# Joining two attention passes into one software pipeline, with the rank projections moved ahead under the convolutions

## The reference

```
# first block; x is normalised, then projected once (weights in_proj)
cq, ckv, kpe, mq, mk, mv, mo, i_pre, f_pre = split(x_normed @ w_in)   # widths 256,128,64,512,512,512,512,4,4
# MLA: 4 heads, causal softmax
q = rms_norm(cq) @ w_uq          # per head 128 "nope" + 64 rotary columns
k, v = rms_norm(ckv) @ w_ukv     # 128 + 128 per head
q_pe, k_pe = apply_rope(q[..., 128:]), apply_rope(kpe)
ctx_mla = causal_mla(q, k, v)
# mLSTM: 4 heads of 128
mq, mk = silu(causal_dwconv(mq)), silu(causal_dwconv(mk))             # 4 taps
h = mlstm_chunkwise(mq, mk, mv, i_pre, f_pre)
h = rms_norm(h per head) * sigmoid(mo)
x = x + post_norm(concat(ctx_mla, h) @ w_out)
```

## Time and profile before

| | |
|---|---|
| Device time, 3 runs | 1392.2 us median (1389.93 to 1393.25) |
| The profiled execution's own time | 1387.27 us |
| Its span, first to last instruction | 1385.3 us |
| Mean granted TensorE clock | 0.983 of full speed |
| PE busy | 95% of the span |
| DVE busy | 57% |
| ACT busy | 40% |
| POOL busy | 3% |

### The profile page before, as it was taken

One profiled execution on the slowest core, in us unless ns is written; L12 is line 12 of the kernel. 1 busy time (PEld: TensorE's weight loads), 2 busy tenths in 40 slices (PEclk: granted clock), 3 DMA queues, 4 the chain that ended last, 5 costly groups with the idle time before them and its releaser, 6 DMA issues.

```text
span 1385.3 us, 17842 instructions
## 1 busy us (share of the span) xinstructions
PE 1316.9 (95%) x6548; PEld 1109.3 (80%) x6548; DVE 784.4 (57%) x1298; ACT 555.7 (40%) x914; POOL 44.9 (3%) x47
## 2 busy tenths in 40 slices
PE   7998879999999999999999999999899999999996
PEld 6877767789888888888777887878798788888886
DVE  5776767556644544222675797586685632355434
ACT  5645545534323223322454654555552322223221
POOL 3000000000000000000021000010000000000002
PEclk9999989999999999999999999999999999999999
DMA  5220110321232233333223232330211232222322
GB/s 177 92 92 16 54 46 16 99 69 61 92 100 97 91 97 113 109 106 106 91 91 107 91 99 84 92 92 31 92 62 61 92 107 91 91 97 100 106 92 76
DMA packets 37101, 120.46 MB, mean 87 GB/s; under 512 B 4508, under 2 KB 6556, under 8 KB 37040
## 3 DMA queue, kind: packets, MB, share of 16 engines
q1 hardware_dynamic: 36464, 117.98, 26.2%
q0 software_dynamic: 576, 1.65, 0.4%
HBM read 112.27 MB, written 2.11 MB: 83 GB/s over the span
## 4 chain that ended last, share of the span: by engine, by line
PE 77%; DVE 14%; ACT 4%; issue 3%; DMA 1%; POOL 0%; POOLq 0%; ACTq 0%; DVEq 0%; SPq 0%
PE bank L779 24%; PE bank L781 24%; PE bank L780 24%; DVE w_lo L1863 3%; DVE tiles L1863 2%; DVE tiles L1866 2%; DVE arena L1863 2%; DVE probsT L1863 1%; PE bank L923 1%; ACT w_hi L1327 1%; PE bank L885 1%; PE bank L876 1%; DVE arena L1866 1%; DVE negmax L2071 1%; ACT arena L1348 1%
## 5 line engine op out<-in xcount | busy, mean ns | idle before, releaser
L1863 DVE TENSOR_TENSOR w_lo<-raw_slab,w_hi 128x1024 fp32r<-128x1024 f32 x199 | 244.3, 1227 | 295.1 <-ACT w_hi L1327 279.7
L779 PE MATMUL bank<-u_hi,w_hi 128*128 128x512 f32 x852 | 337.8, 396 | 14.8 <-DVE tiles L1863 3.8
L781 PE MATMUL bank<-u_hi,w_lo 128*128 128x512 f32 x852 | 334.3, 392 | 0.0
L780 PE MATMUL bank<-u_lo,w_hi 128*128 128x512 f32 x852 | 334.2, 392 | 0.0
L1327 ACT ACTIVATE w_hi<-raw_slab 128x1024 fp32r<-128x1024 f32 x189 | 199.2, 1054 | 183.7 <-PE bank L781 179.9
L779 PE MATMUL bank<-arena,w_hi 128*128 128x512 f32 (+1 forms) x672 | 253.8, 378 | 9.7 <-DVE w_lo L1863 4.9
L780 PE MATMUL bank<-arena,w_hi 128*128 128x512 f32 (+1 forms) x672 | 251.8, 375 | 0.0
L781 PE MATMUL bank<-arena,w_lo 128*128 128x512 f32 (+1 forms) x672 | 251.8, 375 | 0.0
L779 PEld LDWEIGHTS bank<-u_hi,w_hi 128*128 128x128 f32 x852 | 161.2, 189 | 51.7 <-DVE tiles L1863 5.1
L781 PEld LDWEIGHTS bank<-u_hi,w_lo 128*128 128x128 f32 x852 | 161.3, 189 | 34.3
L780 PEld LDWEIGHTS bank<-u_lo,w_hi 128*128 128x128 f32 x852 | 161.4, 189 | 31.8
(11 more groups left out here) (221 smaller groups left out, 1564.7 us busy)
## 6 DMA issues: line engine op xcount, KB each, us to landing
raw_slab<-in_stream SPq DMA_DIRECT2D x207, 512.0 KB, 3.4
arena<-arena SPq DMA_DIRECT2D x32, 128.0 KB, 2.3
residual<-in_xT SPq DMA_DIRECT2D x8, 256.0 KB, 7.8
out_hT<-residual SPq DMA_DIRECT2D x16, 128.0 KB, 1.7
arena<-forget_rows SPq DMA_DIRECT2D x8, 128.0 KB, 2.3
tiles<-in_pT POOLq DMA_DIRECT2D x2, 256.0 KB, 3.0
tiles<-bias_rows POOLq DMA_DIRECT2D x1, 512.0 KB, 3.9
tiles<-in_positions POOLq DMA_DIRECT2D x1, 256.0 KB, 3.5
```

The lines of the kernel that those rows point to most:

```text
L779: pe.matmul(o, ws[0], xs[0], start=first, stop=False)
L780: pe.matmul(o, ws[0], xs[1], start=False, stop=False)
L781: return pe.matmul(o, ws[1], xs[0], start=False, stop=last)
L1863: return nc.vector.tensor_tensor(o, a, b, op)
```

## The change

1. The slabs `kpe` and `gates1` become one, `rg` (gate rows beside the rotary rows). The rotary half-swap, which before was a second set of weight columns, is done by DVE operations that read the other half of the partitions. One slab (24 matmuls) fewer.
2. The stream is now `mv`, `rg`, `cq0`, `cq1`, `ckv`, the eight convolution products in the order of heads (`CONV` = mq0, mk0, mq1, ...), `mo0`: 13 slabs after `mv`. Rank squares, stats and spreads, the rotary tables (`rotary_angles`, ten DVE operations, now before the first norm's `inverse_root`) and the rotary key lie on ACT, DVE and PE among them.
3. The two attentions are one `attention("first")` of 32 units in 38 steps. Fills: halves of `mo1..3` at steps 0 to 5, sixteen expansion products at steps 6 to 13 and 16 to 23, all in PSUM bank 7, one stat of all four mLSTM heads at step 24, four spreads at steps 26 to 29, and 24 matmuls of `out1` at steps 32 to 35. The interlude is gone. MLA's keys and values go to the place of the first block's input (`u_hi`, `u_lo`).
4. Slab conversions in the pipeline follow a table, `FIRST_CONVERT`: at a step it names the slab in use, and the one behind it is converted.

The core of the diff:

```diff
-PHASES = [("mv", 4), ("gates1", 1), ("mq", 4), ("mk", 4), ("mo0", 1), ("mo1", 1), ("mo2", 1), ("mo3", 1),
-          ("cq0", 1), ("cq1", 1), ("ckv", 1), ("kpe", 1), ("uqpe", 1), ("ukv", 1),
-          ("uq", 1), ("out1", KD + 4), ("glu_rest", 2 * KF1 - 4), ("down1", 3 * KD), ("proj", 2), ("ple", KD),
+CONV = [f"m{c}{h}" for h in range(ML_H) for c in "qk"]
+PHASES = [("mv", 4), ("rg", 1), ("cq0", 1), ("cq1", 1), ("ckv", 1)] + [(key, 1) for key in CONV] + [
+          ("mo0", 1), ("mo1", 1), ("mo2", 1), ("mo3", 1), ("exp0", 1), ("exp1", 1), ("exp2", 1), ("out1", KD + 4), ("glu_rest", 2 * KF1 - 4), ("down1", 3 * KD), ("proj", 2), ("ple", KD),
...
-FILLS = {"ml": {step: (key, 0, KD) for step, key in ((0, "mo2"), (1, "mo3"), (17, "cq0"), (18, "cq1"), (19, "ckv"), (20, "kpe"))},
-         "mla": {0: ("qn1", 0, 2), 2: ("qn2", 0, 2), 4: ("qn3", 0, 2)},
+EXPANSIONS = {6: "qpe0", 7: "qpe1", 8: "v0", 9: "v1", 10: "v2", 11: "v3", 12: "kn0", 13: "qn0", 16: "kn1", 17: "qn1",
+              18: "qpe2", 19: "qpe3", 20: "kn2", 21: "kn3", 22: "qn2", 23: "qn3"}
+ML_STAT, ML_SPREAD = 24, 26
+FILLS = {"first": (halves("mo1", 0, 1) | halves("mo2", 2, 3) | halves("mo3", 4, 5) | {step: (key, 0, KD) for step, key in EXPANSIONS.items()}
+                   | {ML_STAT: ("mlstat", 0, KD)} | {ML_SPREAD + h: (f"mlnorm{h}", 0, KD) for h in range(ML_H)}
+                   | {32: ("out1_0", 4, 6), 33: ("out1_0", 6, 8), 34: ("out1_1", 4, 6), 35: ("out1_1", 6, 8)}),
...
+FIRST_CONVERT = {0: "mo1", 2: "mo2", 4: "mo3", 6: "exp0", 12: "exp1", 22: "exp2"}
+SECOND_OUT = 24
...
+        elif key in EXPANDED:
+            n = EXPANDED.index(key)
+            filled = slab(EXPANSION_SLAB[key]) if key in LAST_EXPANSION else (sem.expanded, sum(k not in LAST_EXPANSION for k in EXPANDED[:n + 1]))
+            use(key, STAT_BANK, filled, (sem.rope_read, 2 + int(key[3])) if key[:3] == "qpe" else split(key))
...
                 tt(o, z[:, :], t(RSTD), ALU.mult).then_inc(sem.conv_in, 1)
-                slab_lo(SLAB0["mq"] + n + 1)
...
+                    slab_lo(SLAB0[CONV[n]])
```

More of the change, by code:

```diff
@@ L953, in attention @@
                         last.then_inc(sem.ctx_ready, 1)
[L954 to L959 removed]
+                    if step in FILLS[g]:
+                        fill(*FILLS[g][step])
+            tokens("mv", "mv", fresh=0, norm="attn_pre")
+            every = [u(k) for k in range(KD)]
+            features("rg", arrived("rg"), 0, every).then_inc(sem.slab_used, 1)
+            pe.wait_ge(sem.square_loaded, 16)
+            spread("attn_pre")
             pe.wait_ge(sem.lambda_product, 1)
@@ L987, in ml_score @@
+            features("mo0", arrived("mo0"), 0, every).then_inc(sem.slab_used, 1)
             def ml_score(n, h, i):
@@ L1022, in _, with head_stats @@
-            spread("ml3")
-            uq = arrived("uq")
-            features("qn0", uq, 0, [u(0), u(1)]).then_inc(sem.first_head, 1)
-            def mla_fill(key, first, end):
-                h = int(key[2])
-                features(key, uq, 2 * h, [u(0), u(1)]).then_inc(sem.slab_used if h == MLA_H - 1 else sem.operand_filled, 1)
+            def head_stats(name, squares, done):
+                o = claim(("stat", name))
+                for h in range(4):
+                    pe.wait_ge(sem.sq_done, SQ0[name] + h + 1)
+                    for i in range(ST):
+                        last = pe.matmul(o[:, h * ST + i:h * ST + i + 1], squares(h)[:, i * P:(i + 1) * P], col("one"), start=True, stop=True)
+                    last.then_inc(sem.stat_ready if h == 3 else done, 1)
@@ new lines, in first_fill @@
+            def first_fill(key, first, end):
+                if key in EXPANDED:
+                    expansion(key)
+                elif key == "mlstat":
+                    head_stats("ml", lambda h: early[:, ML_SQ[h]], sem.ml_stat)
+                elif key[:6] == "mlnorm":
+                    if key == "mlnorm0":
+                        pe.wait_ge(sem.rstd_done, NORM_NO["ml"] + 1)
+                    head_spread("ml", int(key[6]), sem.ml_spread)
+                elif key[:4] == "out1":
+                    m = int(key[5])
+                    if first == 4:
+                        claim(("out1", m, 0))
+                        pe.wait_ge(sem.slab_lo, OUT1[m] + 1)
+                    if (m, first) == (0, 4):
+                        pe.wait_ge(sem.ml_lo, ML_H)
+                    o = bank[uses[("out1", m, 0)][0]]
+                    for k in range(first, end):
+                        three(o[:, :], slab(0, out_slot(OUT1, m), k), pair(MIX_HI + k, MIX_LO + k), k == 4, False)
+                else:
+                    projection(key, first, end)
@@ L2194, in ml_gate @@
+            def ml_gate(v):
                 h, i = v // ST, v % ST
```

827 lines of the change are left out of this document (427 added, 400 removed).

## The result

The change made the kernel slower by 0.45%: ratio 1.0045, 95% interval [1.0036, 1.0053], 1396.22 us median of 20 runs against 1389.56 us median of 20 runs before (the three runs shown ahead had 1392.2). The profiled executions are 1395.1 and 1385.3 us in span, 9.8 apart. The forecast was no change, -0.5 us, given as 1391.7.

What follows compares the result with a forecast made beforehand. PE, busy 95% of the span, was taken as the bound. Stretch A 98.4 and B 126.2 start `out1`'s stage 5.4 us later; its terms brought this to about 0, taken as -0.5 on 1392.2: 1391.7 us, range 1373 to 1406.

Steps and rivals of the forecast that it cites:

- stretch B: The 38 pipeline steps: PE work 97.9 us plus losses and low clock, 126.2 us in all.
- the stage of `out1`: Stage behind the pipeline: -5.44 us for moved matmuls, -1.4 for clock, +1 for a conversion, +0.4 for a transfer.
- Conversion behind the product: Convolution loop: PE waits 2.28 us for DVE's take and conversion at each of seven hand-overs, 16.0 us.
- Stretch A: From 33.59 to the end of `mo0`: slabs, waits and low clock, 98.4 us, ending near 132.
- The table loads at step 6: Two loads, four Sigmoids and a conversion on ACT ahead of unit 6's exp, 5.8 us; 4 counted as loss.
- Bank 7 in steps 16 to 23: Expansions wait for bank 7 at every other step, 1.1 to 1.7 us; a loss of 5.3 us.
- rival 3: Bank 7 as a chain: all 16 expansion steps wait 1.2 us, +8, about 1400; chance 0.25 together with rival 2.
- Sum 97.9: PE's work in the 38 pipeline steps, in us, before losses and low clock.
- the clock term: Low clock in the 38 pipeline steps, counted at 4.8 us.
- reservoir: From 33.59 to 252.81 before: some 44 us of waits and low clock, 219.2 us against about 175 of work.
- Rival 1: The pipeline hides the waits and the clock stays up: -13 and -6, about 1373 us; chance 0.28.
- Rival 2: Half clock behind each of the loop's seven waits, DVE's chain 2 us longer: +9, about 1401; chance 0.25 with rival 3.

Runs made afterwards that it cites:

- e1: Changed kernel, but each convolution step converts the next slab on DVE before waiting for the step's product, not behind it; ratio 0.9992 to the kernel before.
- e3: Changed kernel, but the second expansion slab is converted at step 8 instead of step 6; ratio 1.0056 to the kernel before.
- e4: Changed kernel, but the output gates use Tanh instead of Sigmoid, with the half and the one folded into existing operations; ratio 1.0021 to the kernel before.
- e5: Changed kernel, but every other expansion of steps 16 to 23 lies in PSUM bank 6 instead of bank 7; ratio 0.9999 to the kernel before.
- e6: Changed kernel, but the 24 matmuls of `out1` are back in their own stage instead of steps 32 to 35; ratio 1.0051 to the kernel before.
- e9: Changed kernel with e1, e3, e4, e5, `mk0`'s slab converted early, bias product in bank 3, ranks' scaling and splits spread over convolution steps; ratio 0.9848 to the kernel before.

## Why the prediction was wrong, point by point

The step that failed is the pricing of two terms of the sum: PE's own work in stretch B, and the stage of `out1`. The waits in the loop and in the pipeline came at nearly the size that was counted.

- **"Conversion behind the product", 7 x 2.28.** Right. Five waits of 1.92 with a cadence of 7.66 us, 2.2 above the 5.44 of a slab, and at the two others small work lies in the same 2.2. Stretch A was forecast at 98.4 and took 99.35; `mo0` was to end near 132, and step 0 begins at 132.72. e1 shows that this one line of order costs about 7.4 us in the timed runs, more than the 0.45% by which the change lost: with it alone mended the kernel ties with the one before (0.9992).
- **The table loads at step 6.** "I count 4", and PE waited 4.07 (+ 0.70), but not on the path that I had named, the exp of unit 6. It waited for the gate of unit 5, which DVE had behind the conversion of the second expansion slab, and the second table load (1.28) is not on that path. That the figure fits so well is luck. e3 shows that the conversion belonged to this wait, e4 that the loads did: without them the kernel is 3.3 us faster, 2.4 more or less. In the changed kernel the exp starts 0.02 us behind the load's end (160.24 + 1.28 and 161.54). The Trainium skill's price of a drain ("ScalarE: Activation LUTs", "What ACT_TABLE_LOAD costs"), which by an estimate from its 1.38 us would have added 2.8 us, does not show there.
- **Bank 7 in steps 16 to 23.** Right in kind, a little small: 5.3 counted, 6.6 waited, 6.4 gained by a second bank. "Every other step" was about right: five of the eight steps wait. The cause is that neighbouring expansions share one bank, as e5 shows. The Trainium skill's sentence on repeating gaps ("Perfetto Trace Analysis", "Optimization Strategy") names this cause, and the trace agrees, at 0.60 to 2.33 us in five of eight steps and not at rival 3's 1.2 in every one.
- **Mis-sized: "Sum 97.9", the work of PE in stretch B.** This is the first step that failed. B took 131.33 where 126.2 was forecast, though its waits, 23.0 us by the idle times in the trace, are what I had as losses (23.5). PE's busy time in the six windows of B is 108.0, and from start to start without the idle times 108.3. Four stretches of it run at half clock; half of what PE does inside them is 6.3. So the work at full clock is about 102.0, 4.1 more than 97.9, and the clock term was 1.5 short (6.3 for 4.8). The 4.1 are in three places. Stats and spreads were 7.3 instead of 6.4. The 168 matmuls of weights, 3 to 12 at a time between short ones, take 0.252 each by their start times and 0.236 without the half clock, 39.6 us instead of 38.0. The attention units themselves, priced by one mLSTM head and one MLA head at 25.4 + 28.0 = 53.4, come to about 55.2. The kernel before could have shown this. There the same prices add up to "about 175", but the earlier trace rows have 194.2 us of PE busy in the 219.2, and the half clock costs 13.4, worked out the same way: some 181 us of work. So the reservoir was 38 us and not 44.
- **Mis-sized: the stage of `out1`.** Forecast -5.44 for the moved work, -1.4 for the clock and +1.4 for a late conversion and a transfer, -5.4 in all. It took 45.92 against 48.79, -2.9. The clock part came (1.00 instead of 0.97). What is left for the late conversions is 4.0 and not 1.4: idle times of 0.75, 0.22, 0.45 and 1.38, 2.8 in all, and about 1 more in the starts beside them. ACT, in the changed kernel, waits there for the slab from memory each time:

```profile
270.59 1.06 ACT L1402 ACTIVATE arena<-raw_slab 128x1024 fp32r<-128x1024 f32 x1 [1.45 <-DMA raw_slab<-in_stream]
274.02 1.06 ACT L1397 ACTIVATE w_hi<-raw_slab 128x1024 fp32r<-128x1024 f32 x1 [1.40 <-DMA raw_slab<-in_stream]
```

  I had priced the cover that the first two slabs gave by the conversion alone, and not by the load behind it. How much falls to the moved matmuls is not settled: e6 still has a wait of 1.35 at 288.36, and e1, with the matmuls moved, has 0.76, 0.23 and 0.33 and none like the last.
- **Sum.** 0.9 (A) + 5.1 (B) + 2.6 (stage), less 0.2 by which A began earlier, is the 8.4 by which the profile is behind at the stage's end; the forecast's own terms add up to 0. The timed runs say 6.3 (0.45% of 1389.56). All three stretches were forecast too short, and this made "no change" of a loss. The 1396.22 lies inside the band that I gave to no change, 1386 to 1397, but that is luck: the band was laid around a kernel before of 1392.2, and its median over 20 runs is 1389.56. I also had "faster" as the likeliest class, at 0.39, and slower at 0.38.
- **Rival 1** (the pipeline hides it) did not come. e9 is 1.5% faster than the kernel before with the same pipeline of 32 units, so much of the reservoir could be had. How much of that is due to the joined pipeline is not shown: the Tanh gates, for one, could be put into the kernel before too, which has the same two table loads, and that was not tried.
- **Rival 2** came in part. Three of the seven waits of the loop were followed by half clock, and the wait for `mk0` lies in a longer stretch of it, 6.8 us. Together they cost about 7.7, worked out as in stretch B, where 6.2 were counted.

## What to carry to other kernels

When a loop's order is rewritten, count for each conversion which product it stands behind: converting the next slab after the wait for the present one makes PE wait for take and conversion every time, and swapping two lines won back 0.5%. Try the prices of a forecast on the kernel before first: here they gave 175 us for a stretch whose trace has 181. When work is moved as fills into a pipeline, give neighbouring fills different PSUM banks, and look for conversions and table loads that now stand ahead of a gate in the middle of the chain: with a function of the table already loaded (Tanh beside Exp) the loads were gone. Moving such an operation can put it ahead of the next gate, as e3 did, so read the whole list behind its new place. When several terms of a sum nearly cancel, a bias of a few percent in each decides the sign, so the range of the likeliest case must hold them all leaning one way.

## What the runs showed of the hardware

Two waits of PE of 0.89 and 0.73 us were followed by 6.8 us at half clock in one execution (e1), and the same two waits, 14.6 us later in the changed kernel, by full clock. Of the 14.6 us won in the first block some 5 were lost behind it, where e1's execution has 20.5 us at half clock and the changed kernel's 6.8. Exp and Tanh ran with no table load between them in e4, four Tanh of 128x512 in the place of the Sigmoids and in the same time (2.18 and 2.19 us).
